# Where the matmul operands of a float32r hybrid trunk stand in SBUF: block starts and block distances

## What is computed

```python
def swiglu_ffn(h, w_in, w_out):
    gate, up = jnp.split(h @ w_in, 2, axis=-1)          # 1024 -> 2 x 2816
    return (jax.nn.silu(gate) * up) @ w_out             # 2816 -> 1024

h = concatenate([meta, x])                              # (272, 1024)
for i in range(2):
    h = layer_norm(ALPHA * h + 0.5 * swiglu_ffn(h, ffn_w_in[i, 0], ffn_w_out[i, 0]), ...)
    mix = short_conv_mixer(h, ...) if i == 0 else gla_mixer(h, ...)
    h = layer_norm(ALPHA * h + mix, ...)
    h = layer_norm(ALPHA * h + 0.5 * swiglu_ffn(h, ffn_w_in[i, 1], ffn_w_out[i, 1]), ...)
return h[:, 16:]
```

## The kernel before, in words

| tile | start of its first block, mod 256 | from one block to the next |
|---|---|---|
| `weights_hi`, `weights_lo` | 128 | 512 bytes |
| `x_hi` | 128 | 1152 bytes (so 128, 0, 128, ...) |
| `x_lo` | 128 | 1280 bytes (so always 128) |
| `mid_hi`, `mid_lo` | 32 and 160 | 1088 bytes (each block 64 further on) |
| `yc_hi`, `yc_lo` | 192 | 1088 bytes |
| `y_hi`, `y_lo` | 32 | 1024 bytes |
| `zg_hi`, `zg_lo` | 160 and 224 | 1096 bytes (every second block is off a multiple of 16) |

## Time and profile before

### The profile page before, as it was taken

How to read it: one execution, slowest core, us unless ns; L and a number is a source line. 1 busy time by engine, 2 the same in 40 slices (tenths; PEclk the granted TensorE clock), 3 DMA queues, 4 the chain that set the end, 5 groups by cost and what they waited for, 6 DMA issues and landing times.

```text
span 1020.9 us, 18997 instructions
## 1 busy us (share of the span) xinstructions
PE 1009.0 (99%) x7866; PEld 988.4 (97%) x7866; DVE 723.9 (71%) x1078; ACT 512.6 (50%) x746; POOL 122.1 (12%) x136
## 2 busy tenths in 40 slices
PE   9999999999999999999999999999999999999997
PEld 7999999999999999999999999999989999999885
DVE  5856557689889856567697555667897999666444
ACT  6534435464456544444565343444868675444430
POOL 2000003320002000003210000134243320000000
PEclk9999999999999999999999999999999999999999
DMA  9966555637752966556638665555355648865531
GB/s 255 264 189 182 165 169 172 185 99 207 227 167 83 260 174 182 162 168 179 178 115 244 179 175 161 170 162 142 101 137 170 193 117 244 228 194 189 169 122 41
DMA packets 324263, 176.58 MB, mean 173 GB/s; under 512 B 6658, under 2 KB 320048, under 8 KB 324176
## 3 DMA queue, kind: packets, MB, share of 16 engines
q1 hardware_dynamic: 323664, 174.15, 58.8%
q0 software_dynamic: 480, 1.15, 0.4%
q10 hardware_dynamic: 32, 0.07, 0.0%
HBM read 174.29 MB, written 1.05 MB: 172 GB/s over the span
## 4 chain that ended last, share of the span: by engine, by line
PE 92%; DVE 4%; ACT 1%; issue 1%; POOL 1%; POOLq 0%; DVEq 0%; ACTq 0%
PE bank L1295 23%; PE bank L1290 23%; PE bank L1293 23%; PE bank L1309 3%; PE bank L1311 3%; PE bank L1310 3%; PE bank L1453 2%; PE bank L1455 2%; PE bank L1454 2%; PE bank L1335 2%; PE bank L1334 2%; PE bank L1336 2%; DVE weights_lo L806 1%; DVE rms L1203 1%; DVE resid L922 0%
## 5 line engine op out<-in xcount | busy, mean ns | idle before, releaser
L448 ACT ACTIVATE weights_hi<-raw_weights 128x1024 fp32r<-128x1024 f32 x335 | 353.8, 1059 | 414.6 <-PE bank L1295 306.6
L806 DVE TENSOR_TENSOR weights_lo<-raw_weights,weights_hi 128x1024 fp32r<-128x1024 f32 x334 | 415.5, 1250 | 204.9 <-ACT weights_hi L448 203.6
L1290 PE MATMUL bank<-x_hi,weights_hi 128*128 128x272 f32 (+1 forms) x1584 | 227.6, 286 | 0.0
L1295 PE MATMUL bank<-x_lo,weights_hi 128*128 128x272 f32 (+1 forms) x1584 | 227.4, 285 | 0.0
L1293 PE MATMUL bank<-x_hi,weights_lo 128*128 128x272 f32 (+1 forms) x1584 | 225.0, 284 | 0.0
L1295 PEld LDWEIGHTS bank<-x_lo,weights_hi 128*128 128x128 f32 x1584 | 208.0, 188 | 0.0
L1290 PEld LDWEIGHTS bank<-x_hi,weights_hi 128*128 128x128 f32 x1584 | 207.4, 188 | 0.4
L1293 PEld LDWEIGHTS bank<-x_hi,weights_lo 128*128 128x128 f32 x1584 | 206.1, 188 | 0.0
L1290 PE MATMUL bank<-mid_hi,weights_hi 128*128 128x272 f32 x462 | 68.2, 288 | 0.0
L1293 PE MATMUL bank<-mid_hi,weights_lo 128*128 128x272 f32 x462 | 68.1, 288 | 0.0
L1295 PE MATMUL bank<-mid_lo,weights_hi 128*128 128x272 f32 x462 | 68.0, 288 | 0.0
(11 more groups left out here) (231 smaller groups left out, 1198.8 us busy)
## 6 DMA issues: line engine op xcount, KB each, us to landing
raw_weights<-in_ffn_w_in_dram SPq DMA_DIRECT2D x176, 512.0 KB, 4.1
raw_weights<-in_ffn_w_out_dram SPq DMA_DIRECT2D x70, 512.0 KB, 4.0
raw_weights<-in_conv_w_in_dram SPq DMA_DIRECT2D x24, 512.0 KB, 4.1
raw_weights<-in_gla_w_in_dram SPq DMA_DIRECT2D x24, 512.0 KB, 3.9
raw_weights<-in_ffn_w_out_dram SPq DMA_DIRECT2D x24, 384.0 KB, 3.5
raw_weights<-in_conv_w_out_dram SPq DMA_DIRECT2D x8, 512.0 KB, 4.6
raw_weights<-in_gla_w_out_dram SPq DMA_DIRECT2D x8, 512.0 KB, 4.7
x_tok<-in_x_dram SPq DMA_DIRECT2D x2, 512.0 KB, 4.9
```

The lines of the kernel that those rows point to most:

```text
L448: nc.scalar.activation(w_hi[:, n % RING, :], raw[:, n % RAW, :], ACT.Copy).then_inc(hi_split, 1)
L806: nc.vector.tensor_tensor(w_lo[:, s, :], raw[:, n % RAW, :], w_hi[:, s, :].bitcast(F32), ALU.subtract).then_inc(lo_split, 1)
L1290: nc.tensor.matmul(ps, block_of(w_hi, n, k - k0), hi[:, k, cols], start=first and k == k0, stop=False)
L1295: mm = nc.tensor.matmul(ps, block_of(w_hi, n, k - k0), lo[:, k, cols], start=False, stop=last and k == k1 - 1)
```

## The change

The blocks of x, of mid and of the convolution's output get a distance of 1280 bytes (`PITCH`, 320 elements, the next multiple of 64 elements over 272), and small tiles that nothing reads (`pad_x`, 128 bytes; `pad_mid`, 32 bytes) move the first of them to a multiple of 256 bytes. `yc` is made ahead of the convolution's other tiles, so that it takes the start of the shared place, as `y` does. The block distance of `zg` grows from 1096 to 1104 bytes. The room is paid for by `scaled`: it is no longer a tile of its own, and `d_ref` becomes a tile among the attention's.

```diff
+    LINE = 64
+    PITCH = -(-T // LINE) * LINE
...
-        x_hi = sb("x_hi", [P, KD, T + 16], F32R)[:, :, 0:T]
-        x_lo = sb("x_lo", [P, KD, T + 48], F32R)[:, :, 0:T]
+        pad_x = sb("pad_x", [P, LINE // 2])
+        x_hi = sb("x_hi", [P, KD, PITCH], F32R)[:, :, 0:T]
+        x_lo = sb("x_lo", [P, KD, PITCH], F32R)[:, :, 0:T]
...
-        scaled = sb("scaled", [P, 3, T])
...
+        pad_mid = sb("pad_mid", [P, LINE // 8])
...
-            mid_hi = inner.enter_context(nc.sbuf_tensor("mid_hi", [P, KF, T], F32R))
-            mid_lo = inner.enter_context(nc.sbuf_tensor("mid_lo", [P, KF, T], F32R))
+            mid_hi = inner.enter_context(nc.sbuf_tensor("mid_hi", [P, KF, PITCH], F32R))[:, :, 0:T]
+            mid_lo = inner.enter_context(nc.sbuf_tensor("mid_lo", [P, KF, PITCH], F32R))[:, :, 0:T]
...
+            yc_hi = conv.enter_context(nc.sbuf_tensor("yc_hi", [P, KD, PITCH], F32R))[:, :, 0:T]
+            yc_lo = conv.enter_context(nc.sbuf_tensor("yc_lo", [P, KD, PITCH], F32R))[:, :, 0:T]
             cu = conv.enter_context(nc.sbuf_tensor("cu", [P, 2, TAPS - 1 + T], F32))
...
-            yc_hi = conv.enter_context(nc.sbuf_tensor("yc_hi", [P, KD, T], F32R))
-            yc_lo = conv.enter_context(nc.sbuf_tensor("yc_lo", [P, KD, T], F32R))
...
-        d_ref = scaled
+        d_ref = gb("d_ref", [P, 3, T])
...
-            zg_hi = raw_stage.enter_context(nc.sbuf_tensor("zg_hi", [P, KD, T + 2], F32R))
-            zg_lo = raw_stage.enter_context(nc.sbuf_tensor("zg_lo", [P, KD, T + 2], F32R))
+            zg_hi = raw_stage.enter_context(nc.sbuf_tensor("zg_hi", [P, KD, T + 4], F32R))
+            zg_lo = raw_stage.enter_context(nc.sbuf_tensor("zg_lo", [P, KD, T + 4], F32R))
```

## The result

The changed kernel takes 1031.18 us (median of 4 runs, 1028.86 to 1033.3) against 1023.63 (4 runs, 1022.8 to 1024.34): ratio 1.0069 on record, interval 1.0046 to 1.0091. It is slower, and the time lies outside the forecast range of 1011 to 1029. Executions of either kernel come in two lengths 3 to 4.5 us apart, and 1031.18 lies between the two: the changed kernel took 1028.86, 1029.06 and twice 1033.3 us, where the four runs of before were all short, so that short against short the difference is 5.3 us. The profiled execution of before is of the shorter kind and that of after (span 1031.6) of the longer, so that share is taken out first.

A forecast was written before the change was run, and what follows sets the result against it. TensorE's own step, busy 1009.0 of 1020.9 us, was taken to set the time. Terms of -1.4 - 0.2 - 0.4 - 0.5 = -2.5 us took the median from 1023.4 to 1020.9, range 1011 to 1029.

The forecast's parts named there:

- the harsher form: Rival: blocks at 0 and weights at 128 meet badly, 1 ns more on 7700 steps, +7.7 us, 1031; chance 0.07.
- distance costs: Rival: block distance slows x_hi's runs to x_lo's step, +4.0 us; in all +3.1, about 1026.5; slower chance 0.30.
- the last rival: Only moving operands move, weights stay at 128; if relative place counts, nothing is made equal; no chance of its own.
- no change: Rival: place is nothing, group differences come from the order of the products; time stays 1023.4; chance 0.20.
- the slower case: Outcome in which block distance makes x's runs slower, about 1026.5 or, at its harshest, 1031; chance 0.30.
- The step of x: Term for x's 4752 matmuls in runs and some 170 block by block: -0.5 us.
- crossings: Runs going from one kind of place to another make long steps: x -2.0 us; as rival 1012, chance 0.12.
- The ends for x: Bounds of the x term: -2.0 us if x_lo becomes like x_hi, +4.0 if x_hi becomes like x_lo.
- The term of mid: Output projections, 1386 matmuls in runs: 1.0 ns shorter each, -1.4 us; ends 0 and -2.0.
- price per piece of 64 bytes: Loss in TensorE steps over the column time, 0.63 to 0.66 ns per 64 bytes; mid would touch 17 instead of 18.
- The last projection: Term for 264 steps of 233 ns with stationary blocks of mid: 0, ends 0 and -0.2 us.
- zg: Term for zg's 480 matmuls, whose blocks come onto multiples of 16: -0.4 us, ends 0 and -1.0.

## Why the prediction was wrong

That nothing but the step of TensorE counts was right: its waits stayed as they were but for 0.5 us, and the steps add up to the whole difference. Forecast was 1020.9; the case that came was the harsher form of "distance costs", blocks at 0 and weights at 128 meeting badly, which had 0.07. That its 1031 stands so near 1031.18 is luck: its 7.7 us were 1 ns on each of 7700 steps, while the change is 6.2 us as the balance of large terms of both signs, and the median holds a share of the late start. The mechanism is named in the last rival, "the place of the one against the other", but without a price, as falling in with no change or the slower case.

*The step of x failed.* The prediction took "-0.5, near nothing", in us. It was +8.8 at 272 columns and -4.3 at 256, +4.5 in all. The fault was to take x_lo's 1.00 us for the price of its distance or of crossings, and x_hi's 0.99 for what blocks all alike could have. x_hi takes turns (123.5 when all of x does), and x_lo's own place is worth 125.7 when held. Neither row showed place 0 held alike, the one that the change makes; its value, 126.7, lay outside both rows. The ends for x, -2.0 and +4.0 us, were thus too narrow: they took the layouts of before as the ends of what a layout can do. The evenness of x_hi was read from one of its two lines, too; the other, which the earlier trace rows do not show, has the higher median of all three:

```profile
L1290 PE MATMUL bank<-x_hi,weights_hi x216: 283/288/290, 55.3 to 133.6; 128*128 128x272 f32 x108
```

Nor does a duration tell the step: x_hi's steps went from 119 to 129 ns behind its even durations. And 256 columns were expected to "do no better" or follow the others, while they gained 3.6 ns.

*The term of mid had the wrong sign*: -1.4 became +2.2 us. It rested on a price per piece of 64 bytes, 0.63 to 0.66 ns in four groups. That these agreed was chance, by what held places gave: the loss per piece is 0.78 ns with x at 0, 0.59 with x at 64, and 0.44 and 0.83 in 256-column reads at 64 and 128. A read that begins inside a piece paid nothing in mid at 32.

*The last projection*, taken as 0 with -0.2 as its end, gained 1.1 us: the place of a stationary block matters, where the prediction took it that a weight load lies beside the running matmul. *zg*, -0.3 for -0.4, was right; yc (+0.1 for -0.2) and y (+0.6 for 0, of it 0.5 in a wait on VectorE) were small. That the durations of x_lo draw together (287 to 292) came true; that this would be a gain did not.

What stays open: which mechanism makes the reads meet, why turns between 128 and 0 do better than either, why y gained less than x at the same place, whether 256 bytes are the period, and what places off the multiples of 32 would give. Nothing here measured a load of weights alone.

## What to carry to other kernels

Where TensorE is busy all the time with matmuls of 4-byte operands, the place of the moving operand against the stationary one is worth up to 3.3 ns of a step of 124 and 6.2 of one of 117 in this kernel, and 12 of its 1023 us: measure the places in turn, each width by itself, and do not take a round number for a good one. Before a layout is judged by groups of a profile, ask whether any group has it; if none has, the bounds must be wider than the spread of the groups. Tiles that are independent of each other can be tried two at a time in one kernel.

## What the runs showed of the hardware

- At a granted clock of 1.00 the layouts with all blocks alike on multiples of 64 gave eight values, 123.4 to 126.7 ns for 272 columns and 113.7 to 119.9 for 256, by the place of the moving read against the weights. Some come near whole multiples of 8 columns of 0.4167 ns (113.3, 120.0, 123.3 and 126.7 are 272, 288, 296 and 304), but 125.7, 117.8 and 118.7 do not.
- With every block alike and 272 columns, the step does not depend on the tile or the order of the products: x in runs, mid in runs and block by block, and yc block by block gave 126.4 to 126.7 at place 0 and 123.3 to 123.4 at place 64. With 256 columns it does: 113.7 for x in runs and 117.1 for y block by block, both at 192 against the weights.
- The steps are the same whether VectorE and ScalarE are idle or busy, within 0.2 ns (x of 272 columns after the change).
- A stationary block of mid that starts 32 off a multiple of 64 makes a 512-column step 4 to 6 ns longer.
